# Seven block products in place of eight in the up projections of a gated FFN, fp32 split in two parts

## What is computed

```
D_MODEL = 1024; SEQ = 512; FFN_DIM = 2816; CONV_WIDTH = 3
def conv_ffn(h, w_up, conv_w, conv_b, w_down):
    a, u = jnp.split(h @ w_up, 2, axis=-1)
    a = causal_depthwise_conv(a, conv_w, width 3) + conv_b
    return (jax.nn.silu(a) * u) @ w_down
...
h = modulate(x, norm_ffn[i], sh2, sc2)
x = x + g2[:, None, :] * conv_ffn(h, ...)
return rms_norm(x, norm_final)
```

## Time and profile before

| | us |
|---|---|
| median of three runs | 996.33 (992.39 to 997.06) |
| profiled execution, device time | 992.32 |
| profiled execution, span of the trace | 990.1 |
| TensorE busy | 962.0 |
| up stage from its third strip, whole down stage to the last bank | 618.45 to 960 |

### The profile page before, as it was taken

One profiled execution on the slowest core, in us unless ns is written; L12 is line 12 of the kernel. 1 busy time (PEld: TensorE's weight loads), 2 busy tenths in 40 slices (PEclk: granted clock), 3 DMA queues, 4 the chain that ended last, 5 costly groups with the idle time before them and its releaser, 6 DMA issues.

```text
span 990.1 us, 14333 instructions
## 1 busy us (share of the span) xinstructions
PE 962.0 (97%) x5130; PEld 779.5 (79%) x5130; DVE 487.0 (49%) x1098; ACT 393.0 (40%) x705; POOL 12.1 (1%) x31
## 2 busy tenths in 40 slices
PE   6899999999999999999999899999999999999996
PEld 5667887887888878888787788888888888888884
DVE  3343664735736557365573667544444444321214
ACT  6133534435444354353443356433333333311112
POOL 1000000000000000000000002000000000000000
PEclk9999999999999999999999999999999999999999
DMA  9737341443324333333242021433232323223212
GB/s 306 228 109 211 107 149 44 128 128 106 119 71 127 108 93 104 111 117 123 72 120 86 22 86 44 128 97 94 86 105 85 104 86 97 94 87 104 85 64 85
DMA packets 151532, 106.94 MB, mean 108 GB/s; under 512 B 3510, under 2 KB 138830, under 8 KB 151502
## 3 DMA queue, kind: packets, MB, share of 16 engines
q1 hardware_dynamic: 151296, 106.45, 35.4%
q10 hardware_dynamic: 206, 0.08, 0.0%
HBM read 104.42 MB, written 2.10 MB: 108 GB/s over the span
## 4 chain that ended last, share of the span: by engine, by line
PE 91%; DVE 4%; ACT 2%; DMA 2%; SPq 1%; issue 1%; POOL 0%; DVEq 0%; ACTq 0%
PE bank L614 13%; PE bank L616 13%; PE bank L615 13%; PE bank L821 8%; PE bank L823 8%; PE bank L822 8%; PE bank L846 4%; PE bank L845 4%; PE bank L847 4%; PE bank L701 3%; PE bank L677 3%; DMA raw<-in_attn_w_in 2%; PE bank L641 1%; PE bank L634 1%; PE bank L656 1%; PE bank L710 1%
## 5 line engine op out<-in xcount | busy, mean ns | idle before, releaser
L1144 DVE TENSOR_TENSOR wl<-raw,wh 128x1024 fp32r<-128x1024 f32 x144 | 176.0, 1223 | 307.9 <-ACT wh L903 307.4
L903 ACT ACTIVATE wh<-raw 128x1024 fp32r<-128x1024 f32 x144 | 152.6, 1060 | 207.6 <-PE bank L823 112.9
L614 PE MATMUL bank<-hh,wl 128*128 128x512 f32 x544 | 221.1, 406 | 0.0
L616 PE MATMUL bank<-hl,wh 128*128 128x512 f32 x544 | 215.3, 396 | 0.0
L615 PE MATMUL bank<-hh,wh 128*128 128x512 f32 x544 | 215.0, 395 | 0.0
L821 PE MATMUL bank<-fh,wl 128*128 128x512 f32 x336 | 132.9, 396 | 0.0
L822 PE MATMUL bank<-fh,wh 128*128 128x512 f32 x336 | 132.9, 395 | 0.0
L823 PE MATMUL bank<-fl,wh 128*128 128x512 f32 x336 | 132.9, 395 | 0.0
L614 PEld LDWEIGHTS bank<-hh,wl 128*128 128x128 f32 x544 | 102.5, 188 | 26.0 <-issue 3.5
L616 PEld LDWEIGHTS bank<-hl,wh 128*128 128x128 f32 x544 | 102.2, 188 | 24.6
L615 PEld LDWEIGHTS bank<-hh,wh 128*128 128x128 f32 x544 | 102.4, 188 | 21.7
(11 more groups left out here) (172 smaller groups left out, 1078.5 us busy)
## 6 DMA issues: line engine op xcount, KB each, us to landing
raw<-in_attn_w_in SPq DMA_DIRECT2D x72, 512.0 KB, 3.8
raw<-in_ffn_w_up SPq DMA_DIRECT2D x44, 512.0 KB, 3.8
ada_raw<-in_w_ada SPq DMA_DIRECT2D x16, 1024.0 KB, 5.9
raw<-in_ffn_w_down SPq DMA_DIRECT2D x22, 512.0 KB, 3.3
ada<-in_w_ada SPq DMA_DIRECT2D x16, 256.0 KB, 6.9
raw<-in_attn_w_out SPq DMA_DIRECT2D x8, 512.0 KB, 3.6
x_nat<-in_x SPq DMA_DIRECT2D x4, 512.0 KB, 5.3
x_nat<-in_w_ada SPq DMA_DIRECT2D x8, 256.0 KB, 6.0
```

Source lines behind the costliest of these rows:

```text
L614: nc.tensor.matmul(bank[:], wl[:, slot, t], xh[:, t], start=(t == 0), stop=False)
L616: last = nc.tensor.matmul(bank[:], wh[:, slot, t], xl[:, t], start=False, stop=(t == KT - 1))
L903: nc.scalar.activation(dst, src, ACT.Copy).then_inc(done, 1)
L1144: nc.vector.tensor_tensor(dst, src, high.bitcast(F32), ALU.subtract).then_inc(done, 1)
```

## The change

Tiles 0 to 2 (`PLAIN = 3`, six strips) stay as they are. For tiles 3 to 21 the two strips of a tile are taken as one product of a 2x2 block matrix of weights (gate or linear strip; first or last 512 input features, `HK = 4` tiles) with a 2x2 block matrix of input (features; first or last 256 tokens), and worked with seven block products (Strassen's scheme in Winograd's form). Each product is 4 tiles times 3 parts, 12 matmuls of 256 columns, so 84 matmuls of 256 columns stand where 48 of 512 stood.

For that the input is also needed as four sums of blocks (`t32`, split into `th`, `tl`; each 128x1024), made once, two on VectorE and two on GpSimd, out of a float32 copy `h2` of the input. GpSimd completes that copy with eight additions. And for every tile GpSimd makes four sums of weight blocks (`sums`, 128x512 each), which are split in two pieces of 128x1024; the first strip is split whole (128x1024), of the second only its last half (128x512). ScalarE copies three partial results out of PSUM, VectorE adds three (`gate_sum` for the gate branch, `up_late` for the linear branch of the late tokens). The taps now read `gate_sum` in SBUF. The product of the branches goes to `act_v` in float32 for all tiles and is split in the down stage, in a ring of four (`split_act`). The loads get a third and a fourth buffer (`raw[:, 2]`, `raw_up`), and both strips of a tile are loaded at once. `y_bank` takes another order of banks, and the host's size of a DMA scratch area is set to 2048.

The core of the diff:

```diff
+PLAIN = 3
+FORMS = 4
+PRODUCTS = 7
+HK = KT // 2
+ACT_RING = 4
...
         def y_bank(o):
-            return banks[(o + 4) % 8]
+            return banks[(3, 7, 0, 1, 2, 6, 5, 4)[o]]
...
+            def load_up(f, w):
+                sp.wait_ge(fl_ready, forms_before(f - 1))
+                sp.wait_ge(sums_done, 4 * (f - PLAIN - 1))
+                for u in range(2):
+                    sp.dma_start(up_raw(w)[u], up_columns(f, u)).then_inc(fraw_in[2 * w + u], 16)
...
+            pool.wait_ge(h2_done, KT)
+            pool.wait_ge(tail_done, 2 * (OUT_STRIPS - OUT_AHEAD))
+            nc.gpsimd.tensor_tensor(t32[:, 2], h2[:, HK:KT, HALF:T], h2[:, 0:HK, HALF:T], ALU.subtract).then_inc(t34_done, 1)
+            pool.wait_ge(t12_done, 2)
+            nc.gpsimd.tensor_tensor(t32[:, 3], h2[:, HK:KT, 0:HALF], t32[:, 1], ALU.subtract).then_inc(t34_done, 1)
+            def sum_up(f, w, value):
+                first, second = up_raw(w)
+                pool.wait_ge(fraw_in[2 * w], value)
+                pool.wait_ge(fraw_in[2 * w + 1], value)
...
+                    pool.wait_ge(fl_ready, forms_before(f - 1) + 1)
...
+                nc.gpsimd.tensor_tensor(sums[:, 0], second[:, 0:HK], second[:, HK:KT], ALU.add).then_inc(sums_done, 1)
+                pool.wait_ge(sums_done, done + 1)
+                nc.gpsimd.tensor_tensor(sums[:, 1], sums[:, 0], first[:, 0:HK], ALU.subtract).then_inc(sums_done, 1)
+                if not (isinstance(f, int) and f == PLAIN):
+                    pool.wait_ge(fl_ready, forms_before(f - 1) + 3)
+                nc.gpsimd.tensor_tensor(sums[:, 2], first[:, 0:HK], second[:, 0:HK], ALU.subtract).then_inc(sums_done, 1)
+                pool.wait_ge(sums_done, done + 2)
+                nc.gpsimd.tensor_tensor(sums[:, 3], first[:, HK:KT], sums[:, 1], ALU.subtract).then_inc(sums_done, 1)
...
+            def up(f, w, m):          # TensorE
+                r, q, z = banks[4 * w], banks[4 * w + 1], banks[4 * w + 2]
+                pe.wait_ge(fl_ready, forms_before(f) + 2)
+                pe.wait_ge(gated, f - 1)
+                product(r, 0, 0, fh[:, 0:HK, early], fl[:, 0:HK, early], True, False)
+                product(q, 1, 0, th[:, 0], tl[:, 0], True, False)
+                pe.wait_ge(copied, 3 * (f - PLAIN) + 1)
+                product(r, 1, 1, th[:, 1], tl[:, 1], False, False)
+                product(z, 0, 1, fh[:, HK:KT, early], fl[:, HK:KT, early], True, True)
+                pe.wait_ge(fl_ready, forms_before(f) + 3)
+                pe.wait_ge(copied, 3 * (f - PLAIN) + 3)
+                product(r, 2, 0, th[:, 2], tl[:, 2], False, False)
+                product(q, 2, 1, fh[:, HK:KT, late], fl[:, HK:KT, late], False, True)
+                pe.wait_ge(fl_ready, forms_before(f) + 4)
+                pe.wait_ge(added, 3 * (f - PLAIN) + 2)
+                product(r, 3, 0, th[:, 3], tl[:, 3], False, True)
...
+                    if static and k == 0:          # TensorE, down(0)
+                        if o == 2:
+                            pe.wait_ge(gated, FT - 1)
+                        if o == 5:
+                            pe.wait_ge(added, 3 * (FT - PLAIN))
+                        if o == 7:
+                            pe.wait_ge(gated, FT)
...
+            def up(f, w, m):          # ScalarE
+                    act.wait_ge(added, 3 * (f - PLAIN))
+                    last_tap(f - 1, gate_sum[:])
+                split_last(split_h, ...)
+                copy_product(f, 1, r, p1_copy)
+                    make_gate(f - 1)
+                copy_product(f, 2, q, p5_copy)
+                copy_product(f, 3, r, u2_copy)
+                if not final:
+                    split_sums(split_h, f + 1, 0, (prod_done, done + 3), fh_ready, wh)
+                    split_direct(split_h, f + 1, 1 - w, loads_next(f, w, m), (prod_done, done + 4), fh_ready, wh)
+                    split_sums(split_h, f + 1, 1, (prod_done, done + 6), fh_ready, wh)
+                else:
+                    for k in range(3):
+                        split_act(split_h, k, k, act_h_done, act_h)
+                        split_down(split_h, k, k, k // 2, fh_ready, wh)
```

More of the change, by code:

```diff
@@ L338, in split_ffn, with forms_before, up_raw @@
[L338 to L344, removed]
+        def forms_before(f):
+            return 2 * PLAIN + FORMS * (f - PLAIN)
+        ALL_FORMS = 2 * PLAIN + FORMS * (FT - PLAIN)
+        def up_raw(f):
+            return (raw[:, 0], raw[:, 1]) if f % 2 == 0 else (raw[:, 2], raw_up[:])
@@ L459, in _ @@
+            for u in range(2):
+                sp.dma_start(raw[:, u].rearrange("p t n -> p (t n)"), w_down[u]).then_inc(fraw_in[u], 16)
+            with sp.Fori(1, FT // 2) as m:
+                for u in range(2):
+                    src = w_down[columns(sp, 2 * m + u, 1)].rearrange("a p n -> p (a n)")
+                    sp.wait_ge(fl_ready, ALL_FORMS + 2 * m + u - 1)
                     sp.dma_start(raw[:, u].rearrange("p t n -> p (t n)"), src).then_inc(fraw_in[u], 16)
-            sp.wait_ge(act_l_done, FT)
@@ L825, in _ @@
-            up(0)
-            with pe.Fori(1, FT // 2) as i:
-                up(i)
+            for j in range(2, 2 * PLAIN):
+                high, low = plain_slot(j)
+                bank = banks[j % 4]
+                pe.wait_ge(fl_ready, j + 1)
+                if j >= 4:
+                    pe.wait_ge(gated, 1)
+                for t in range(KT):
+                    nc.tensor.matmul(bank[:], low[:, t], fh[:, t], start=(t == 0), stop=False)
+                    nc.tensor.matmul(bank[:], high[:, t], fh[:, t], start=False, stop=False)
+                    last = nc.tensor.matmul(bank[:], high[:, t], fl[:, t], start=False, stop=(t == KT - 1))
+                last.then_inc(fstrip_done, 1)
@@ new lines, in product @@
+            def product(bank, slot, late, xh, xl, fresh, final):
+                for t in range(HK):
+                    high, low = wh[:, slot, HK * late + t], wl[:, slot, HK * late + t]
+                    nc.tensor.matmul(bank[:, 0:HALF], low, xh[:, t], start=(fresh and t == 0), stop=False,
+                                     skip_group_check=True)
+                    nc.tensor.matmul(bank[:, 0:HALF], high, xh[:, t], start=False, stop=False, skip_group_check=True)
+                    last = nc.tensor.matmul(bank[:, 0:HALF], high, xl[:, t], start=False, stop=(final and t == HK - 1),
+                                            skip_group_check=True)
+                last.then_inc(prod_done, 1)
```

395 lines of the change are left out of this document (268 added, 127 removed).

## The result

| | before | after |
|---|---|---|
| median, us | 996.60 (992.39 to 997.09, 7 runs) | 1002.47 (1001.07 to 1004.26, 7 runs) |
| ratio to before, 95% interval | | 1.007 (1.0051 to 1.009) |
| profiled execution (span), us | 992.32 (990.1) | 1004.19 (1002.4) |

The changed kernel is slower by 0.7%. The ratio is taken over all seven runs of each (their means are 7.0 us apart, the two medians 5.9). The forecast was 990, faster by 0.6%: the time lies in the range, the sign is wrong.

A forecast was written before the change was run, and what follows sets the result against it. The prediction took TensorE's matmuls to bound the kernel before, VectorE with its holds to set the new loop's pace. Its terms, -21.1 + 7.5 + 4.3 + 3.4 = -5.9 us off 996.33, gave 990, range 978 to 1008.

The forecast's parts named there:

- Matmuls, −21.1: TensorE in the up stage: 84 matmuls of 256 columns for 48 of 512, 1.11 us less per tile, 21.1 for 19.
- VectorE's own 7.4 a tile: Product loop: VectorE's own operations need 7.4 us of a tile's 10.08, holds by GpSimd not counted.
- The hold, 1.05 for 512 elements: A VectorE operation with two SBUF inputs waits for GpSimd's first 1.05 us, of 1.27; four per tile, up to 4.2.
- About 1.0 of the holds was hidden: Product loop: about 1.0 us of holds per tile falls beside PSUM reads, giving 10.6 a tile, 0.5 over TensorE's 10.08.
- 10.9 as the point from which the kernel is slower: Product loop: the kernel ends slower once VectorE with its holds needs over 10.9 us a tile, 0.3 above the forecast 10.6.
- a walk through three tiles: Product loop: three tiles followed in the assumed order of GpSimd's pairs, finding about 1.0 us of holds hidden.
- The head start, −2: VectorE starts the loop about 2 us ahead, taken off 19 x 0.5; the loop's loss is 7.5 us.
- Start, +4.3: Before the first product of the new form: TensorE waits from 640.85 to 645.0 for copy, load, sums and splits, 4.3 us.
- End, +3.4: End of the up stage: down tile 0's eighth bank waits for the last product of the branches, 3.4 us.
- Down stage, nothing: Down stage: an added 128x512 split on each engine per tile, 0.6 and 0.6 of 5.6 us, costs nothing.
- VectorE is the bound: Rival: whole-operation holds of 1.27 or slower GpSimd sums give VectorE 11.8 us a tile, 1010 us in all; chance 0.20.
- everything hidden: Rival: GpSimd's sums fall where VectorE waits or reads PSUM, so VectorE needs at most 10.08 a tile, 983 us; chance 0.22.

The follow-up runs named there:

- e1: Changed kernel with GpSimd's four sums per tile in tiles 4 to 21 made on 8 elements instead of 512; 981.70 us, ratio 0.9859 to the kernel before.
- e2: As e1, with a GpSimd memset of 128x1024, which reads nothing, behind each small sum; 980.82 us, ratio 0.9862 to the kernel before.
- e5: Changed kernel with the splits for down tile 2 put behind the last tile's taps, SiLU and product; 998.23 us, ratio 1.0039 to the kernel before.
- e3: Changed kernel with the sums of tiles 4 to 21 made by VectorE instead of GpSimd; 980.58 us, ratio 0.9864 to the kernel before.
- e8: Changed kernel with GpSimd's third and fourth sum per tile waiting for VectorE's product of the branches of tile f - 2; 1002.61 us, ratio 1.0071.

## Why the prediction was wrong

Step by step, by its own terms:

- **Matmuls, −21.1.** Right. The steps in a product are 0.118 apart (0.120 forecast), a tile 9.94 where nothing holds it up (10.08 forecast), so 23.7 were to be had.
- **VectorE's own 7.4 a tile.** Right: 7.37 in e1.
- **The hold, 1.05 for 512 elements, shorter than GpSimd's operation.** Right: 1.10, of 1.30. GpSimd's time was forecast at 1.27. The tap that starts at 772.96 ends at 774.58, and less its own 0.75 it was let in at 773.83, 1.10 behind GpSimd's start at 772.73, with GpSimd busy to 774.03. The Trainium skill (SBUF — State Buffer, "SBUF: two separate sides") has the loser blocked for the whole instruction; by these rows VectorE loses 0.2 us less than that (no row tells whether it is let in earlier or does some of its own start while it waits). That only reads of GpSimd's hold it is what e2 shows, and the Trainium skill has it too (SBUF — State Buffer, "Who interferes with whom").
- **"About 1.0 of the holds was hidden": the step that failed.** 4 x 1.05 = 4.2 was the full price and 3.95 was paid, so 0.25 was hidden (0.45, if each hold is priced at the measured 1.10). The prediction had the first sum start "around the third addition", some 5 us behind the half split. The load lands later: the half split ends at 766.69, the two loads are issued at 766.87 and 767.43, and the sum starts at 772.73, 6.0 us behind, when the third addition (771.33) is over and 0.23 ahead of the taps. The second pair then follows without a pause. 7.37 + 3.95 = 11.3 is the measured 11.28, against 10.6 forecast. Over the 17 tiles that lose, (11.27 − 10.6) x 17 = 11.4. The text itself had named 10.9 as the point from which the kernel is slower, 0.3 above its own number, and that number rested on a walk through three tiles whose phase no row gave. The alternating rhythm of the first tiles, 10.97, is nearer to it; an estimate for a loop that keeps it, 17 x 0.30 = 5 us less than 1002.5, is still no faster than before.
- **The head start, −2.** About right in size, but from another place: the first tile and the last lose nothing, 2 x (11.27 − 9.94) = 2.7. In all the loop was forecast at −21.1 + 7.5 = −13.6 and took −0.2: 11.4 of that from the holds, 1.5 from the clock (below).
- **Start, +4.3.** 3.9 of wait, 4.1 with what lies around it. Right, and so is the chain: GpSimd's first two sums at 639.18 and 640.55, VectorE's splits held to 2.17 and 2.28:

```profile
643.84 2.17 DVE L1367 TENSOR_TENSOR wl<-sums,wh 128x1024 fp32r<-128x1024 f32 x1
645.94 2.28 DVE L1367 TENSOR_TENSOR wl<-raw,wh 128x1024 fp32r<-128x1024 f32 x1
```

- **End, +3.4.** 3.2, by the route forecast: ScalarE waits for the load of down tile 2, and the taps, SiLU and product come behind it:

```profile
863.87 1.06 ACT L1082 ACTIVATE wh<-raw 128x1024 fp32r<-128x1024 f32 x1 [3.90 <-DMA raw<-in_ffn_w_down]
```
```profile
869.14 0.50 PE L1024 MATMUL bank<-act_h,wl 128*128 128x512 f32 x1 [3.16 <-DVE act_v L1652]
```

- **Missing: the clock behind the two waits.** 1.5 inside the loop (17 steps from 648.75 to 652.28 in 3.53 instead of 17 x 0.118 = 2.0) and 1.5 in down tile 0. e5, which takes the wait at the end away, takes the half clock with it.
- **Down stage, nothing.** Right apart from that.

The rival "VectorE is the bound" has the right mechanism (VectorE full, TensorE at the seventh product) at too high a price: 11.8 a tile, measured 11.28. Its reason, a hold for the whole operation, is not what happened; nearly nothing being hidden was enough. The rival "everything hidden" gave 983; the changed kernel is not that case, but e1 and e3, which take the holds away, measure 981.7 and 980.6.

One reading ahead of the prediction was loose: the stretch from 618.45 to 864.80, told as the up stage, holds two tiles of the down stage as well, since the first matmul of the down stage is at 853.64. Both parts run at full clock without a gap, so no term changes.

Left open: whether all four sums could be moved so that they fall beside VectorE's PSUM operations. That needs earlier loads, and e8 moved only two of them; it wasn't tried. The activations' split in the down stage was not run alone. The medians leave 3 of the traces' 8.9 us unaccounted for, within the spread of the runs. And nothing here shows what ends the alternating rhythm of the loop.

## What to carry to other kernels

An engine's idle time in the profile before is only a budget for its own instructions: an operation of GpSimd that reads SBUF cost VectorE, when it met one with two SBUF inputs, 1.10 us, more than the 0.68 that VectorE needs to do the same work. So price an offload at what it takes from the neighbour, assume that nothing is hidden unless the trace gives the phase of the load that starts it, and where the forecast stands 0.3 us a tile from its turning point, say the sign is open. And a removed product pays only as far as the next engine follows: moving the sums to VectorE and two pieces of work at the ends made the same scheme 2.0% faster than before instead of 0.7% slower (with the sums alone moved, e3, 1.4% faster).

## What the runs showed of the hardware

- GpSimd's reads, not its writes, hold VectorE: 4 fills of 0.95 us a tile cost nothing, 4 sums of 1.30 cost 3.95.
- It works both ways: a sum of 1.30 takes 1.75 beside VectorE's two-input operations and 2.27 beside a split of 1.21 (e8, 766.90).
- A wait of TensorE of 3 to 4 us cost more than itself. In the changed kernel the granted clock fell from 1.00 to 0.50, that is from 2.4 to 1.2 GHz, some 0.5 us after work resumed at the start and 1.5 us after it at the end (steps of 0.43 us instead of 0.233), and was back 3.5 us later: 1.5 us lost each time. In e3, behind the wait of 3.3 at the end, it was at half as soon as work resumed and for 6.05 us, and 2.8 were lost. The waits of up to 1.0 in each tile left the clock at 1.00 in the stretch from 761 to 781, and so did e5's wait of 0.5 at the end.
